# Two hybrid layers on one core: float32 sums of squares, the next head's masking ahead of the head's merge, weight turns behind the second panel

## The reference: what is computed

```python
q = rope(rmsnorm(two_map_heads(aq), q_norm_g), cos, sin)   # 8 heads, 2 maps, 64 wide
k = rope(rmsnorm(two_map_heads(ak), k_norm_g), cos, sin)
...
    sc = einsum(q, k) * scale
    p = softmax(where(causal, sc, -inf))
    a = p[map 0] - lam * p[map 1]
    out = einsum(a, v)
oa = rmsnorm(out, attn_norm_g) * (1.0 - lam_init) * silu(az)
```

## Time and profile before

| | before |
|---|---|
| median of 3 runs | 3386.95 us (3380.55 to 3393.57) |
| profiled execution, its own time | 3382.91 us |
| its span | 3381.1 us |
| PE busy | 3251.9 us, 96% of the span |
| DVE / ACT / POOL busy | 1437.8 / 820.0 / 1821.1 us |
| granted TensorE clock, mean | 0.986 |

### The profile page before, as it was taken

How to read it: one execution, slowest core, us unless ns; L and a number is a source line. 1 busy time by engine, 2 the same in 40 slices (tenths; PEclk the granted TensorE clock), 3 DMA queues, 4 the chain that set the end, 5 groups by cost and what they waited for, 6 DMA issues and landing times.

```text
span 3381.1 us, 47060 instructions
## 1 busy us (share of the span) xinstructions
PE 3251.9 (96%) x15456; PEld 2691.9 (80%) x15456; DVE 1437.8 (43%) x2325; ACT 820.0 (24%) x1773; POOL 1821.1 (54%) x1028
## 2 busy tenths in 40 slices
PE   5998999998998999999999999999899999999998
PEld 4877888886777888878887887888788888878887
DVE  7777462117776642126666112111166662121011
ACT  4554332014554331022222002101122220021020
POOL 3444455663444555655455665666554555656664
PEclk9999999999999999999999999999999999999999
DMA  3222222222221222232222222222222222222322
GB/s 106 75 89 67 69 75 81 98 98 63 87 87 57 76 73 89 98 102 84 75 84 78 90 96 88 94 99 95 83 84 84 75 83 87 99 87 94 99 93 99
DMA packets 87983, 290.54 MB, mean 86 GB/s; under 512 B 12833, under 2 KB 13537, under 8 KB 87921
## 3 DMA queue, kind: packets, MB, share of 16 engines
q1 hardware_dynamic: 75024, 273.12, 24.3%
q10 hardware_dynamic: 12896, 16.64, 1.8%
HBM read 275.00 MB, written 2.10 MB: 82 GB/s over the span
## 4 chain that ended last, share of the span: by engine, by line
PE 87%; DVE 7%; issue 3%; ACT 1%; ACTq 1%; DVEq 0%; DMA 0%
PE bank L556 27%; PE bank L558 27%; PE bank L557 27%; PE bank L624 1%; DVE xq L1416 1%; PE bank L742 1%; PE bank L605 1%; PE bank L653 1%; DVE k_hi L1347 1%; ACTq L1032 1%; PE bank L775 1%; DVE xk L1416 1%; DVE xn L1356 0%; DVE xk L1412 0%; PE bank L715 0%
## 5 line engine op out<-in xcount | busy, mean ns | idle before, releaser
L537 POOL TENSOR_SCALAR w_hi<-raw 128x1024 fp32r<-128x1024 f32 x512 | 560.6, 1095 | 1493.7 <-DMA raw<-in_w_in 1026.9
L540 POOL TENSOR_TENSOR w_lo<-raw,w_hi 128x1024 fp32r<-128x1024 f32 x512 | 1260.4, 2462 | 42.7
L556 PE MATMUL bank<-h_lo,w_hi 128*128 128x512 f32 x2816 | 1118.4, 397 | 0.6 <-DVE h_lo L1359 0.3
L558 PE MATMUL bank<-h_hi,w_hi 128*128 128x512 f32 x2816 | 1099.9, 391 | 0.0
L557 PE MATMUL bank<-h_hi,w_lo 128*128 128x512 f32 x2816 | 1098.7, 390 | 0.0
L558 PEld LDWEIGHTS bank<-h_hi,w_hi 128*128 128x128 f32 x2816 | 530.4, 188 | 113.2
L556 PEld LDWEIGHTS bank<-h_lo,w_hi 128*128 128x128 f32 x2816 | 531.4, 189 | 108.8 <-issue 2.5
L557 PEld LDWEIGHTS bank<-h_hi,w_lo 128*128 128x128 f32 x2816 | 531.6, 189 | 106.0
L1373 DVE TENSOR_TENSOR x<-x,bank 128x512 f32 x64 | 44.0, 688 | 458.1 <-PE bank L558 458.1
L556 PE MATMUL bank<-w_lo,up_hi 128*128 128x512 f32 x512 | 199.2, 389 | 0.0
L557 PE MATMUL bank<-w_hi,up_lo 128*128 128x512 f32 x512 | 199.2, 389 | 0.0
(11 more groups left out here) (297 smaller groups left out, 4520.1 us busy)
## 6 DMA issues: line engine op xcount, KB each, us to landing
raw<-in_w_in SPq DMA_DIRECT2D x288, 512.0 KB, 3.3
raw<-in_w_up SPq DMA_DIRECT2D x64, 512.0 KB, 3.3
raw<-in_w_down SPq DMA_DIRECT2D x64, 512.0 KB, 3.2
raw<-in_w_out_a SPq DMA_DIRECT2D x16, 512.0 KB, 3.2
raw<-in_w_out_b SPq DMA_DIRECT2D x16, 512.0 KB, 3.3
raw<-in_w_o SPq DMA_DIRECT2D x16, 512.0 KB, 3.2
raw<-in_p_ret SPq DMA_DIRECT2D x16, 512.0 KB, 3.3
raw<-in_p_sb SPq DMA_DIRECT2D x16, 512.0 KB, 3.3
```

Of the source, the lines that this page charges most:

```text
L537: nc.gpsimd.tensor_scalar(m.w_hi[:, slot], m.raw[:, slot], 1.0, 0.0, ALU.mult, ALU.add).then_inc(s["w_step"], 1)
L540: nc.gpsimd.tensor_tensor(m.w_lo[:, slot], m.raw[:, slot], m.w_hi[:, slot].bitcast(F32), ALU.subtract).then_inc(s["split"], 1)
L556: nc.tensor.matmul(dst, hi, rhs_lo, start=first, stop=False, **more)
L558: return nc.tensor.matmul(dst, hi, rhs_hi, start=False, stop=last, **more)
```

## The change

Four things change, all in the attention of the first block.

1. The squares are no longer split. `grp` becomes float32, and `group_sum` multiplies float32 squares: for k one 128x512 float32 matmul, for q four float32 matmuls with the squares as the stationary side and two columns of `grp` as the moving one, which give the sums by token (128 tokens x 2 maps, for 4 blocks).
2. q is no longer multiplied with its factors. `group_rstd(0)` makes them from 128x8 sums (Ln, Exp and a Copy that scales), and `maxima` takes them as the scale of each row. ACT does this ahead of the transfers for k's rotation.
3. DVE masks the next head's scores (`masked`, with `maxima` in the order of query blocks 3, 2, 1, 0) ahead of `head_branch`, and `combine` goes by halves (blocks 3 and 2, then 1 and 0).
4. On PE all three `weight_turns` stand behind the gemm of the second panel and q's group sum, and all `values` behind the third panel and k's group sum.

```diff
-        order = (3, 1, 2, 0)
+        order = (3, 2, 1, 0)
+        halves = ((3, 2), (1, 0))
...
             def group_sum(which, ahead):
 
-                lo, hi = ((m.sql_q, m.sqh_q), (m.sql_k, m.sqh_k))[which]
-                pe.wait_ge(s["sq_split"], at.at("a", ahead, times=2) + (which + 1))
+                pe.wait_ge(s["sq_ready"], at.at("a", ahead, times=2) + (which + 1))
                 misc_bank()
-                nc.tensor.matmul(misc[:], m.grp[:], lo[:], start=True, stop=False)
-                nc.tensor.matmul(misc[:], m.grp[:], hi[:], start=False, stop=True).then_inc(s["ss_done"], 1)
+                if which == 1:
+                    mm = nc.tensor.matmul(misc[:], m.grp[:], m.sq_k[:], start=True, stop=True)
+                else:
+                    for b in range(TB):
+                        mm = nc.tensor.matmul(misc[:, 2 * b:2 * b + 2], m.sq_q[:, b * P:b * P + P], m.grp[:, 0:P:64],
+                                              start=True, stop=True)
+                mm.then_inc(s["ss_done"], 1)
...
                 with at.loop(A_HEADS - 1, panel=4, acc=4, a=1, misc=4):
                     scores()
                     h_gemm()
-                    weight_turns(0)
                     h_gemm()
                     group_sum(0, 1)
-                    weight_turns(1)
-                    values(0)
-                    weight_turns(2)
+                    for g in range(len(groups)):
+                        weight_turns(g)
                     h_gemm()
                     group_sum(1, 1)
-                    values(1)
-                    values(2)
+                    for g in range(len(groups)):
+                        values(g)
                     value_turns(1)
...
             def group_rstd(which, sq_buf, ahead):
                 act.wait_ge(s["ss_done"], at.at("a", ahead, times=2) + (which + 1))
-                own(activation(sq_buf[:], misc[:], ACT.Ln, bias=m.col[:, 2:3], scale=1.0 / A_DH))
-                act.sem_inc(s["misc_free"], 1)
-                activation(sq_buf[:], sq_buf[:], ACT.Exp, scale=-0.5).then_inc(s["rstd_ready"], 1)
+                if which == 1:
+                    own(activation(sq_buf[:], misc[:], ACT.Ln, bias=m.col[:, 2:3], scale=1.0 / A_DH))
+                    act.sem_inc(s["misc_free"], 1)
+                    activation(sq_buf[:], sq_buf[:], ACT.Exp, scale=-0.5).then_inc(s["rstd_ready"], 1)
+                else:
+                    rows = m.sm[:, 84:92]
+                    own(activation(rows, misc[:, 0:2 * TB], ACT.Ln, bias=m.col[:, 2:3], scale=1.0 / A_DH))
+                    act.sem_inc(s["misc_free"], 1)
+                    own(activation(rows, rows, ACT.Exp, scale=-0.5))
+                    activation(rows, rows, ACT.Copy, scale=-(A_DH ** -0.5)).then_inc(s["rstd_ready"], 1)
...
                     qk_out(0, m.xq, m.sq_q)
-                    turned_out(0)
                     rotate_halves(m.rot_q, m.xq, s["rot_q_in"], 32)
                     qk_out(1, m.xk, m.sq_k)
+                    group_rstd(0, m.sq_q, 1)
                     rotate_halves(m.rot_k, m.xk, s["rot_k_in"], 32)
-                    group_rstd(0, m.sq_q, 1)
-                    turned_out(1)
-                    turned_out(2)
+                    for g in range(len(groups)):
+                        turned_out(g)
                     copy_out(m.vT, s["vT_ready"])
                     group_rstd(1, m.sq_k, 1)
...
-            def split_squares(which, ahead):
-                dve.wait_ge(s["sq_ready"], at.at("a", ahead, times=2) + (which + 1))
-                hi, lo, sq_buf = ((m.sqh_q, m.sql_q, m.sq_q), (m.sqh_k, m.sql_k, m.sq_k))[which]
-                split(hi[:], lo[:], sq_buf[:], s["sq_split"])
-
             def rotate_qk(which, ahead):
                 x, rot, sqb = ((m.xq, m.rot_q, m.sq_q), (m.xk, m.rot_k, m.sq_k))[which]
                 dve.wait_ge(s["rot_k_in" if which else "rot_q_in"], at.at("a", ahead + 1, times=64))
                 rotate(x, rot, m.cos, m.sin,
-                       (sqb, (s["rstd_ready"], at.at("a", ahead, times=2) + (which + 1))))
+                       (sqb, (s["rstd_ready"], at.at("a", ahead, times=2) + 2)) if which else None)
                 hi, lo = ((m.q_hi, m.q_lo), (m.k_hi, m.k_lo))[which]
                 split(hi[:], lo[:], x[:], s["qk_ready"])
...
-            def maxima(i):
+            def maxima(i, ahead):
 
                 qb = order[i]
-                if i < 3:
-                    dve.wait_ge(s["scores_done"], at.at("a", times=3) + (i + 1))
+                if i < 2:
+                    dve.wait_ge(s["scores_done"], at.at("a", ahead, times=3) + (1, 3)[i])
                     dve.sem_inc(s["rows_begun"], 1)
                 for k, p in enumerate((m.p0, m.p1)):
                     ins = nc.vector.tensor_tensor_reduce(
                         p[:, QOFF[qb]:QOFF[qb] + (qb + 1) * P], sq[k][qb], m.mq_row[:, (TB - 1 - qb) * P:],
-                        op0=ALU.add, op1=ALU.min, scale=-(A_DH ** -0.5), scalar=-BIG_NEG,
-                        accum_out=m.sm[:, 20 + 2 * i + k:21 + 2 * i + k])
+                        op0=ALU.add, op1=ALU.min, scale=m.sm[:, 84 + 2 * qb + k:85 + 2 * qb + k], scalar=-BIG_NEG,
+                        accum_out=m.sm[:, 20 + 2 * qb + k:21 + 2 * qb + k])
                 ins.then_inc(s["max_ready"], 1)
 
-            def combine(i):
-
-                qb = order[i]
-                dve.wait_ge(s["p_ready"], at.at("a", times=TB) + (i + 1))
-                l0, ratio = m.sm[:, 28 + 2 * i:29 + 2 * i], m.sm[:, 44 + i:45 + i]
-                own(nc.vector.reciprocal(m.sm[:, 36 + 2 * qb:38 + 2 * qb], m.sm[:, 28 + 2 * i:30 + 2 * i]))
-                own(stt(ratio, l0, m.prm[:, NEG_LAMBDA:NEG_LAMBDA + 1], m.sm[:, 37 + 2 * qb:38 + 2 * qb],
+            def combine(half):
+
+                dve.wait_ge(s["p_ready"], at.at("a", times=TB) + 2 * (half + 1))
+                lo = halves[half][1]
+                sums, inverse = m.sm[:, 28 + 2 * lo:32 + 2 * lo], m.sm[:, 36 + 2 * lo:40 + 2 * lo]
+                own(nc.vector.reciprocal(inverse, sums))
+                own(stt(m.sm[:, 44 + lo:46 + lo], sums.rearrange("p (b k) -> p b k", k=2)[:, :, 0],
+                        m.prm[:, NEG_LAMBDA:NEG_LAMBDA + 1], inverse.rearrange("p (b k) -> p b k", k=2)[:, :, 1],
                         ALU.mult, ALU.mult))
-                w = slice(QOFF[qb], QOFF[qb] + (qb + 1) * P)
-                stt(m.p0[:, w], m.p1[:, w], ratio, m.p0[:, w], ALU.mult, ALU.add).then_inc(s["a_ready"], 1)
+                for qb in halves[half]:
+                    w = slice(QOFF[qb], QOFF[qb] + (qb + 1) * P)
+                    stt(m.p0[:, w], m.p1[:, w], m.sm[:, 44 + qb:45 + qb], m.p0[:, w], ALU.mult,
+                        ALU.add).then_inc(s["a_ready"], 1)
+
+            def masked(ahead):
+
+
+                dve.wait_ge(s["pv_done"], at.at("a", ahead + 1))
+                dve.wait_ge(s["rstd_ready"], at.at("a", ahead, times=2) + 1)
+                for i in range(TB):
+                    maxima(i, ahead)
 
             def weights():
-
-
-                dve.wait_ge(s["pv_done"], at.at("a", 1))
-                for i in range(TB):
-                    maxima(i)
-                for i in range(TB):
-                    combine(i)
+                for half in range(2):
+                    combine(half)
...
                 take_panel()
                 take_panel()
                 take_panel()
-                split_squares(0, 0)
-                split_squares(1, 0)
                 rotate_qk(0, 0)
                 rotate_qk(1, 0)
+                masked(0)
                 with at.loop(A_HEADS - 1, panel=4, acc=4, a=1, own=DVE_A) as i:
                     weights()
                     take_panel()
                     take_panel()
                     take_panel()
-                    split_squares(0, 1)
-                    split_squares(1, 1)
                     rotate_qk(0, 1)
                     rotate_qk(1, 1)
                     head_normalised()
                     head_gate()
+                    masked(1)
                     head_branch(i)
```

More of the change, by code:

```diff
@@ L177 @@
 PE_MISC_L2 = 20
-ACT_L1 = 133
-ACT_A = 8
+ACT_L1 = 141
+ACT_A = 9
 ACT_B = 10
@@ L182 @@
 ACT_R = 7
-DVE_L1 = 335
-DVE_A = 22
+DVE_L1 = 279
+DVE_A = 15
 DVE_B = 28
@@ L242, in __init__ @@
         self.ident = place.put("ident", [P, P])
-        self.grp = place.put("grp", [P, P], F32R)
+        self.grp = place.put("grp", [P, P])
         self.col = place.put("col", [P, 8])
@@ L306, in __init__ @@
         self.p1 = place.put("p1", [P, TRI])
-        self.sqh_q = place.put("sqh_q", [P, S], F32R)
-        self.sqh_k = place.put("sqh_k", [P, S], F32R)
         place = Region(nc, o_u, o_rest)
@@ L378, in __init__ @@
         self.mm1 = place.put("mm1", [P, S])
-        place = Region(nc, o_u + 2 * S * 4, o_rest)
-        self.sql_q = place.put("sql_q", [P, S], F32R)
-        self.sql_k = place.put("sql_k", [P, S], F32R)
         place = Region(nc, o_u, o_rest)
@@ L413 @@
```

(6 more changed lines are left out.)

## The result

| | before | changed |
|---|---|---|
| median of 5 runs | 3389.21 us (3380.55 to 3393.57) | 3363.93 us (3358.7 to 3369.9) |
| ratio, 95% interval | | 0.9931 [0.9915, 0.9947] |
| profiled execution's span | 3381.1 us | 3367.7 us |
| PE busy | 3251.9 us | 3263.4 us |

The kernel is 0.7% faster (0.53% to 0.85%), about 25 us between the medians. The two profiled executions lie only 13.4 us apart: the one before was 6 us under its median, the changed one 6 us over its own.

A forecast was written before the change was run, and what follows sets the result against it. PE was taken to wait for `o_sb` behind DVE's queue. Waits and clock falls saved (-30.4 us) plus PE's added work (+13.2) gave -17.2, from 3382.9 to 3365.7 us, stated as 3366; range over all cases 3352 to 3382.

The forecast's parts named there:

- The mechanism: At a turn's end PE waits for `o_sb`, late through DVE's queue beside POOL's operations: 21.6 us in 13 waits.
- PE's own work: PE in a loop turn: 29.66 us before, 0.87 more with the float32 sums, 30.53 us; 13.2 us added in all.
- The size on record: Whole kernel: waits and clock falls -30.4 us, PE's added work +13.2, net -17.2 us.
- First turns: `o_sb` waits of 21.6 us were taken as gone, except 2.1 us kept at the last heads.
- first rival: xk's product starts 0.6 us later, behind `w_hi`'s start; it and `k_hi` are held, `o_sb` at 31.0; chance 0.27.
- Last heads: At a layer's last head 2.1 us of `o_sb` wait stays; of two weights waits only about 1.1 us comes back.
- The clock: Four turns with a fall to clock 0.50 behind an `o_sb` wait: 4 x 1.7, 6.8 us saved.
- its own signs: Trace checks, including turns of 30.4 to 30.6 us, `o_sb` waits over 0.2 us only at last heads, `maxima` behind first scores.
- The margin: At a turn's end `o_sb` is done at 29.9 us, 0.6 us ahead of PE at 30.53.
- small-wait rival: DVE stays held by POOL; PE waits 0.5 us for `o_sb` each turn; net -8 us, 3375; chance 0.27.
- cheap-sums rival: q's eight loads hide, costing 0.3 us a turn instead of 0.88; net -26 us, 3357; chance 0.16.
- slower case: DVE's `head_branch` ahead of `combine`, held by POOL, makes the weights late, beyond 3.4 us of cover; chance 0.05.

The follow-up runs named there:

- short w_lo: Kernel before, with POOL's second operation on each panel replaced by a shorter one-input zero fill, leaving out the weights' low part: 3327.4 us, one run.
- q's sums twice: Changed kernel with the four float32 matmuls of q's sums issued twice, same result written twice: 3382.3 us, one run.
- the sums alone: Kernel before with only the unsplit float32 sums of squares (one 128x512 matmul each for q and k), old order: 3372.6 us, ratio 0.9967 to before.
- logs-late kernel: Changed kernel with masking behind `head_branch` again and ACT's three gate-row activations moved from before the first turn to before the last head: 3352.3 us, 0.9886 of before.
- the turns alone: Kernel before with only PE's order changed: all weight turns behind the second gemm, all values behind the third: 3379.4 us, one run.
- the masks back: Changed kernel with masking again behind `head_branch`, at the start of the next turn: 3357.9 us, ratio 0.9925 to before.

## Why the prediction came out as it did

**The mechanism** was right: DVE's chain behind POOL's holds made `o_sb` late (short w_lo shows it), and with the chain shortened PE fills the turn. What decides now is PE's own work (q's sums twice). The parts differ in worth, though. Into a turn, `o_sb` was done at 31.07 us before, at 30.91 with the sums alone, at 30.47 with the turns moved as well, and at 29.62 with the row scale too (the masks made no difference to it): the row scale did most, the time freed on DVE by the sums hardly any. The sums fill PE's wait with 0.74 us of work. The move of the turns also keeps PE from waiting at L666, and the masks brought nothing.

**The size on record**, -17.2 us, is the 17.3 us that the two attention stretches show in the profiles, but by errors that cancel:

- *PE's own work.* The turn is 30.01 us, not 30.53. The sums cost 0.40 (k) and 0.34 (q) more than before, together 0.74 instead of 0.88. The rest is in the base: 29.66 was the turn less the idle time as listed, 1.57, but that is counted from a modelled end; the last gemm matmul started at 220.16, its successor would have followed 0.23 later, at 220.39, and the real wait was 1.73. Without a stop, `output_turns` also pass on to `scores` 0.12 us sooner. These three make 0.42 of the 0.52 us a turn; the last 0.1 is not traced. 0.5 us in 12 turns: 6 us better than forecast.
- *First turns.* The sum took all `o_sb` waits as gone. One stays in the first turn of each layer, 3.1 us in all, close to the first rival's pattern: ACT came late from the gate rows, xk's product began at 91.43, behind `w_lo`'s start at 90.78, and took 2.61 us (`k_hi` behind it was free, 0.43). The logs-late kernel shows the cause.
- *Last heads.* I gave back 2.1 us there, and set the waits at L706 aside as lying "behind the last head". They lie ahead of its `output_turns` and end the step. PE waits for `erow`, and DVE gets to it in one unbroken run. In the first layer `a_hi`, now ahead of `combine`, was held 1.63 us; the first operation on the gate rows started 12.1 us into the step instead of 10.6, and `erow`'s last one on DVE ended at 21.5 instead of 19.8. L666 waits 2.25 and 0.58 us, and 1.98 in the second layer, but L706 behind it would have taken that time anyway. The last step takes 24.0 and 23.6 us against 22.2 and 22.1: 3.2 us more, nearly all that the removed waits ahead of it (1.6 and 1.7 us) had cost, and 1.1 us worse than forecast.
- *The clock.* I priced four falls at 6.8 us. Three of them stood in loop turns, the fourth at the second layer's last head. In the two attention stretches together the clock stood at 0.50 for 27.0 us before and for 17.5 us now: by estimate 4.7 us back, 2.1 less than forecast. Three short falls remain, behind the first-turn wait of 1.6 us and the last heads' waits at L666. With the turns alone, 12 waits of about 1.4 us stand in the profile and none of them has a fall behind it; with the sums alone 14 of 0.8, and none. So waits of this length sometimes have one behind them and often don't; only the stretches themselves can be priced, not each wait.

From 17.2 us that makes 6 better, then 3.1, 1.1 and 2.1 worse: 16.9, beside the 17.3 measured. (The sum also took 1.5 us for `k_lo` where its row says 1.7.) That the sum met the stretches is luck in part. The forecast of 3366 us against 3364 measured is so twice over, since it was reckoned from an execution 4 us under the median then known; from the median itself the same sum gives 3370. Of its own signs three failed: turns of 30.4 to 30.6 us (30.0), no wait for `o_sb` but at last heads (one in each first turn), and no stretch at clock 0.5 at a loop turn's start (one, at 828.4).

**The margin.** `o_sb` was to come 0.6 us early and comes 0.4 early; the small-wait rival (0.27) came true only in the first turns. The cheap-sums rival fell: 0.1 us a record is right even for two columns, with float32 and with fp32r (0.09). The slower case did not come about in the loops, but its mechanism, `head_branch` held ahead of `combine`, is what the last heads pay for. The page SBUF — State Buffer of the Trainium skill (section "Who interferes with whom") calls the hold an exclusive lock that the first one gets for the whole instruction; the trace agrees: a four-element product took 1.27 us and ended 0.02 us behind `w_lo`.

**What stays open.** The medians differ by 25 us, the attention stretches of the profiles by 17, the spans by 13. The 12 us between the first and the last are where the two profiled executions lie: 6 us under the one median, 6 us over the other. The rest of the program does the same work. The clock bears on it: the mean granted clock was 0.987 to 0.989 in the five runs of the changed kernel (0.987 in the profiled one, the slowest of them), and 0.984 to 0.988 in the 37 runs of the kernel before that stand beside the experiments, on three chips. One fall of 3.4 us takes 0.0005 off the mean, so the means differ by some four falls, an estimated 7 us, of which the stretches hold part. What sets off the falls outside the stretches was not shown.

## What to carry to other kernels

Where two engines hold each other, look at the order in time of their single operations and not at their busy shares: an engine busy for 43% of the span set the turn, and moving three activations out of the first turn decided whether 1.6 us were lost at its end. Ask of each wait whether a later one would take up its time: at the last head the wait for the weights did not count, the one for `erow` behind it did. Take a part out of a change one at a time: here one of four parts brought nothing and cost at the loop's end, and two edits beside it (the masks back, those three activations moved) bring another 0.4%. A turn's own work is the difference of starts in an undisturbed stretch, not its length less the listed idle time.

## What was unexpected of the hardware

- Two-column matmuls with a full 128x128 stationary side cost 0.10 to 0.11 us a record in float32 (8 records in 0.80 us, 8 more in 0.89) and 0.09 in fp32r (4 in 0.36). Four float32 ones (0.80 us) cost nearly as much as one float32 matmul of 512 columns (0.86).
- The clock fell to 0.50 for 3.4 us behind 4 of 13 waits of 1.3 to 1.95 us in one kernel and behind none of 12 such waits in another.
- A VectorE product of 4 elements a partition took 1.27 us beside GpSimd's `w_lo` and ended 0.02 us behind it; where nothing held it, it took 0.16.
- Masking with a row scale read from SBUF takes 0.75 us for 512 columns against 0.68 with a constant.
